# One GpSimd addition in place of two for both heads of a forgetting-attention key tile

## What is computed

```python
logits = jnp.einsum('bthd,bshd->bhts', qi, k).astype(jnp.float32) * ATTN_SCALE
logits = logits + (ci[..., :, None] - c_key[:, :, None, :])
logits = jnp.where(pi[:, None] >= key_pos[None, :], logits, NEG_INF)
probs = jax.nn.softmax(logits, axis=-1)
return jnp.einsum('bhts,bshd->bthd', probs.astype(v.dtype), v)
```

```python
merged = (jax.nn.sigmoid(ga + b_gate[i, 0]) * (y_swa @ w_up_swa[i])
          + jax.nn.sigmoid(gf + b_gate[i, 1]) * (y_fox @ w_up_fox[i]))
h = h + _rmsnorm(merged @ w_out[i], g_post[i])
```

## Time and profile before

| | |
|---|---|
| median of three executions | 843.04 us |
| the three | 843.82, 837.07, 843.04 us |
| the profiled execution | 837.59 us, of it the span from first to last instruction 835.8 us |
| mean granted TensorE clock | 0.992 |

### The profile page before, as it was taken

The page is one execution under the profiler, slowest core; times in us unless marked ns, Lnnn a source line. Parts: engine busy times, 40 slices in busy tenths (PEclk is TensorE's granted clock), DMA queues, the critical chain, the costliest instruction groups (busy, mean ns, idle before and its releaser), DMA issues.

```text
span 835.8 us, 12898 instructions
## 1 busy us (share of the span) xinstructions
PE 802.9 (96%) x4514; PEld 649.0 (78%) x4514; DVE 505.1 (60%) x1050; ACT 315.3 (38%) x645; POOL 350.8 (42%) x292
## 2 busy tenths in 40 slices
PE   3999999999999999999999999999989999999997
PEld 3999999987878878788787865756565688878885
DVE  7944788456676767645646457795878744442222
ACT  6422241333333333333333336666667123222111
POOL 4412224454445435344444324757774344412221
PEclk9999999999999999999999999999998999999999
DMA  9342424569857346355364599999700475342221
GB/s 295 103 127 53 128 65 109 135 164 267 240 164 205 103 140 191 103 165 165 99 178 116 138 239 237 235 240 226 188 2 2 138 224 150 118 174 103 87 91 75
DMA packets 122712, 125.00 MB, mean 150 GB/s; under 512 B 30116, under 2 KB 92404, under 8 KB 122648
## 3 DMA queue, kind: packets, MB, share of 16 engines
q1 hardware_dynamic: 121208, 119.92, 53.7%
q10 hardware_dynamic: 1440, 4.26, 1.4%
HBM read 90.93 MB, written 34.92 MB: 151 GB/s over the span
## 4 chain that ended last, share of the span: by engine, by line
PE 83%; DVE 6%; issue 5%; POOL 3%; ACT 1%; DMA 1%; DVEq 0%; SPq 0%; ACTq 0%; POOLq 0%
PE PS L1857 20%; PE PS L1858 20%; PE PS L1859 20%; PE PS L2106 4%; PE PS L2107 3%; PE PS L2108 3%; PE PS L1964 2%; POOL acc L1220 2%; PE PS L2029 1%; PE PS L2009 1%; PE PS L2044 1%; PE PS L2059 1%; PE PS L2010 1%; PE PS L1879 1%; DMA x_all<-in_x_dram 1%
## 5 line engine op out<-in xcount | busy, mean ns | idle before, releaser
L1151 POOL TENSOR_TENSOR ops<-s_sum,ops 128x512 fp32r<-128x512 f32 x64 | 87.5, 1378 | 111.2 <-ACT ops L1249 111.2
L1857 PE MATMUL PS<-t_hi,ops 128*128 128x512 f32 x256 | 101.1, 395 | 0.0
L1858 PE MATMUL PS<-t_lo,ops 128*128 128x512 f32 x256 | 99.8, 390 | 0.0
L1859 PE MATMUL PS<-t_hi,ops 128*128 128x512 f32 x256 | 99.8, 390 | 0.0
L1151 POOL TENSOR_TENSOR ops<-raw,ops 128x512 fp32r<-128x512 f32 x48 | 65.5, 1365 | 69.0 <-ACT ops L1249 68.9
L1220 POOL TENSOR_TENSOR acc<-acc,p_fox 128x400 f32<-128x400 f32 (+5 forms) x76 | 62.2, 838 | 5.9 <-ACT p_fox L1373 3.6
L1172 POOL TENSOR_TENSOR w_plain<-raw,w_plain 128x1024 fp32r<-128x1024 f32 x10 | 28.0, 2796 | 84.8 <-ACT w_plain L1278 84.8
L1679 DVE TENSOR_TENSOR z_tmp<-u,PS 128x512 f32<-128x512 f32 x48 | 33.0, 686 | 49.2 <-PE PS L1859 28.2
L1249 ACT ACTIVATE ops<-s_sum 128x512 fp32r<-128x512 f32 x64 | 39.6, 623 | 52.8 <-DVE s_sum L1481 41.8
L1373 ACT ACTIVATE p_fox<-PS,neg_c_col 128x512 f32<-128x512 f32 (+5 forms) x112 | 54.2, 534 | 14.0 <-PE PS L2015 7.5
L1859 PEld LDWEIGHTS PS<-t_hi,ops 128*128 128x128 f32 x256 | 48.1, 188 | 10.6
(11 more groups left out here) (205 smaller groups left out, 2176.9 us busy)
## 6 DMA issues: line engine op xcount, KB each, us to landing
raw<-in_w_in_dram SPq DMA_DIRECT2D x34, 512.0 KB, 5.2
q_dram<-stage_b SPq DMA_DIRECT2D x32, 256.0 KB, 3.0
g_dram<-stage_b SPq DMA_DIRECT2D x32, 256.0 KB, 2.0
tanh_g<-g_dram SPq DMA_DIRECT2D x16, 512.0 KB, 3.9
max_k<-k_dram SPq DMA_DIRECT2D x16, 260.0 KB, 5.5
max_c<-neg_c_dram SPq DMA_DIRECT2D x8, 520.0 KB, 6.2
x_all<-in_x_dram SPq DMA_DIRECT2D x8, 512.0 KB, 7.9
raw<-in_w_in_dram SPq DMA_DIRECT2D x16, 256.0 KB, 4.7
```

Source lines behind the costliest of these rows:

```text
L1151: nc.gpsimd.tensor_tensor(ops[:, i % OPS, 1], op_source(p, name), ops[:, i % OPS, 0].bitcast(F32), ALU.subtract).then_inc(op_ready, 1)
L1857: pe.matmul(dst, hi_w, hi, start=first, stop=False)
L1858: pe.matmul(dst, hi_w, lo, start=False, stop=False)
L1859: return pe.matmul(dst, lo_w, hi, start=False, stop=last)
```

## The change

In a unit that isn't shared, GpSimd now handles both heads with one instruction: the two blocks of `acc` and the two neighbouring tiles of the `p_fox` ring are addressed as one operand of two rows. It waits for both heads' exponentials. Shared units are as they were. The counts in `acc_done` follow: a unit with one instruction for both heads counts once, and both its `p_fox` tiles become free with it.

```diff
                 for h in range(2):
-                    who = "dve" if h and st["q"] and st["i"] <= 4 else "pool"
-                    acc_total[who] += 1
+                    shared = st["q"] and st["i"] <= 4
+                    who = "dve" if h and shared else "pool"
+                    acc_total[who] += 1 if shared or not h else 0
...
-                    for h in range(2):
-                        n = 2 * u + h
-                        if acc_by[n] != "pool":
-                            continue
-                        dst = acc[0:keys, f % 2, h, c0:c0 + w]
+                    n = 2 * u
+                    pool.wait_ge(fox_exp, n + 1)
+                    if q == 1 and i <= 4:
+                        dst = acc[0:keys, f % 2, 0, c0:c0 + w]
                         tile = p_fox[0:keys, n % PT_RING, 0:w]
-                        pool.wait_ge(fox_exp, n + 1)
-                        if q == 0 and i == 0:
-                            nc.gpsimd.tensor_copy(dst, tile).then_inc(acc_done["pool"], 1)
-                            continue
-                        other = p_fox[:, (n - 2) % PT_RING, :] if (q, i) == (1, 1) else dst
-                        if n in acc_before:
-                            pool.wait_ge(*acc_before[n])
-                        nc.gpsimd.tensor_tensor(dst, other, tile, ALU.add).then_inc(acc_done["pool"], 1)
+                        other = p_fox[:, (n - 2) % PT_RING, :] if i == 1 else dst
+                    else:
+                        pool.wait_ge(fox_exp, n + 2)
+                        if n + 1 in acc_before:
+                            pool.wait_ge(*acc_before[n + 1])
+                        dst = acc[0:keys, f % 2, :, c0:c0 + w]
+                        tile = p_fox[0:keys, n % PT_RING:n % PT_RING + 2, 0:w]
+                        other = dst
+                    if i == 0:
+                        nc.gpsimd.tensor_copy(dst, tile).then_inc(acc_done["pool"], 1)
+                        continue
+                    if n in acc_before:
+                        pool.wait_ge(*acc_before[n])
+                    nc.gpsimd.tensor_tensor(dst, other, tile, ALU.add).then_inc(acc_done["pool"], 1)
```

## The result

| | kernel before | changed kernel |
|---|---|---|
| median of 22 runs | 838.10 us | 841.60 us |
| lowest to highest | 835.63 to 843.82 | 839.58 to 846.29 |
| span of the profiled execution | 835.8 us | 840.2 us |

The ratio is 1.0041, with a 95% interval from 1.0025 to 1.0057: the changed kernel is slower by 0.4%, or 3.4 us of 838 (2.1 to 4.8 by the interval). That is within the 1% called no change ahead of the result, to which 0.90 was given, and yet larger than the uncertainty of this many runs; 841.6 lies in the range of 837.0 to 849.0. A second measurement of the unchanged pair of kernels gave 1.0040 (1.0011 to 1.0069).

The account below looks back on a forecast made before the run. PE was taken to bound the kernel, waiting mainly for DVE, with GpSimd having some 49 us to spare in attention. 1.2 + 0.6 + 0.2 - 0.1 = +1.9 us on the 843.04 us median gave 844.9 us, range 837.0 to 849.0.

Parts of the forecast that it names:

- What bounds the kernel: Attention: PE is bound and lacks DVE's results; of GpSimd's 2.4 us net saving only 0.1 us counts, at `probs`.
- The price of a pair: GpSimd: one instruction for 2 x 400 columns takes 1.90 us (bounds 1.76 and 2.06) instead of 2.02 for two.
- 621 to 625 us: DVE's `y` split and small operation wait longer behind GpSimd's pairs; PE's 1.91 us pause grows by 1.2 us.
- 645 to 651 us: Before the merge part, the `y` split PE waits for ends later behind a pair: +0.6 us (+0.4 to +0.7).
- The ring: `p_fox` tiles freed together could hold up ACT, tightest at 528 us; cost nothing, covered by an existing wait.
- The wait for both heads: Pairs wait for head 1's exponential, one ACT operation later; cost nothing, covered by `probs`' wait for `rec`.
- 585.6 us: DVE's small operation, blocked by both heads' 144 columns instead of one's, delays the `y` PE awaits: +0.2 us.
- The sum: Whole kernel: 1.2 + 0.6 + 0.2 - 0.1 = +1.9 us, 844.9 us against the median of 843.04.
- The saved time arrives: Rival: PE's pauses hang on GpSimd, so 2.4 to 5.8 us are saved, 837.2 to 840.6 us; chance 0.18.
- DVE blocked everywhere: Rival: pairs double all blocks of DVE's small operations and splits, up to +11.0 us, 854.0 us; chance 0.04.
- Hidden anyway: Rival: PE's pauses shift into each other and the delay disappears, 843.0 us; chance 0.18.
- The slow clock stays longer: Rival: PE's longer pause near 625 us brings 3 to 6 us more half clock, 846.4 to 847.9 us; chance 0.15.

Follow-up runs that it names:

- e6: Kernel before with only the 27 pairs of j = 0 to 2 merged, the last pair of heads left as two instructions: 839.34 us, ratio 0.9997.
- e10: Kernel before with pairs merged only in j = 1, j = 2 and the second half of j = 0, first `y` split two key tiles later: 839.17 us, 1.0005.
- e1: Changed kernel with its joint waits and counts kept, but two GpSimd instructions for a pair again: 840.97 us, ratio 1.0030 to the kernel before.
- e8: Changed kernel with the first split of `y` issued two key tiles later: 839.31 us, ratio 1.0003 to the kernel before.
- e2: Kernel before with only the nine pairs of the last two heads (j = 3) merged: 840.92 us, ratio 1.0033.
- e11: Kernel before with only the first split of `y` two key tiles later, measured a second time: 838.19 us, ratio 0.9984.
- e7: Kernel before with only the first split of `y` two key tiles later, first measurement: 839.04 us, ratio 0.9990.

## Why the prediction was right, and where not

**What bounds the kernel, and that GpSimd's saving is worth nothing on the path:** right. With 27 of 36 pairs merged (e6) or 22 of them (e10) the kernel is no faster. GpSimd's time fell by 4.7 us, where 4 to 6 were forecast, but that it fits is luck: its copies and additions alone went from 72.5 to 65.9 us, 6.6 less, and 1.8 us came back in the projections (L1173), which the change does not touch. In the second profile, without this, its time is 7.1 us lower. The 0.1 us that PE was to gain at its wait for `probs` did not come: it waits 0.28 us there in both kernels.

**The price of a pair:** right. 1.90 us were taken for 2 x 400 columns, and 1.88 to 1.90 us measured where nothing disturbs it; the 544 columns take 1.35 us, so 256 columns more cost 0.54 to 0.56 us, 2.1 to 2.2 ns each. A dependent pair starts 0.23 us after the end of the one before it, where 0.15 had been read from single additions. It happens seven times in each of the two profiles, not ten.

**621 to 625 us, +1.2 us:** right in mechanism and order of the turns, 1.07 us in size. The split was put at about 2.6 us and took 2.58, the pause at 3.1 us and it was 2.98. e1 takes the long hold away and has the 1.90 us of before.

**645 to 651 us, +0.6 us:** right in mechanism, +0.46 us in size. The early split came 0.36 us sooner (forecast 0.3), and the blocked one took 2.18 us and set the start of the merge part.

**The ring, nothing:** right in the changed kernel. At 528 ACT no longer waits, and its waits for `acc` in attention fell from 4.2 to 3.5 us in all. At the end the joint return does delay ACT's last exponentials, so that PE stands 0.46 us longer ahead of the last value matmuls. The forecast did not have this. It stays without effect because the split comes later still. e1 shows the cost when it is not covered: a wait of 2.16 us instead of 0.58.

**The wait for both heads, nothing:** this step failed, a term put at nothing by a cover that is not there at the start. The cover named was `probs`' wait for `rec`. At the start of attention there is no such wait ahead of the first tiles: GpSimd stands idle and takes each exponential as it comes. The copy of two rows starts one exponential later, two dependent starts follow, and the pair is still running when DVE's copies come. That is +0.5 us, measured as 0.52 to 0.65 in all six kernels that merge there or wait jointly, and 0.00 to 0.01 in all five others. The sentence "where GpSimd is there first" named the condition; the place was in the rows from 494 us on, ahead of the stretch that was read.

**585.6 us, +0.2 us:** open. It is +0.34 us in one profile of the changed kernel and in those of e6, e8 and e10, and -0.08 in the other profile of the changed kernel. The pair that DVE met was that of 2 x 272 columns, not that of 2 x 144 which the forecast named.

**The sum.** By the parts 1.9 us were forecast; the three places measure 2.1 us, which is the lower end of what the ratio gives, 2.1 to 4.8. That the two sums agree is partly luck: 0.5 us at the start that had been left out stands against smaller terms elsewhere. Between the 2.1 us and the 3.4 us of the ratio 1.3 us stay open.

The mean clocks say where they may lie. A mean clock lower by 0.0029 over 840 us is some 4.9 us more at half clock in a run, about one and a half stretches of 3.4 us. At 0.9 to 1.6 us for a stretch, as measured below, that is an estimate of 1.3 to 2.3 us. Among the 93 runs of the kernel before, a run with a clock lower by 0.001 is longer by 1.0 us on average, but pauses and slow stretches come together, so that this does not tell cause from effect. Nor do clock and time always go together: e2 has a ratio of 1.0033 with a clock of 0.9903, near that of before. So the slow clock is a likely part of the open 1.3 us and is not shown to be all of it.

The absolute forecast missed by only 3.3 us because two errors partly cancel: it was set on the median of three runs, 4.9 us above that of 22, and the growth was put 1.6 us too small. 838.1 + 1.9 would have been 840.0.

**The rivals.** "The saved time arrives" and "DVE blocked everywhere" did not happen: the small operations take 12.9 us in all where it was 13.0, and the seven long splits 12.4 where it was 10.4. "Hidden anyway" is excluded by the interval. "The slow clock stays longer" did not happen behind the pause itself: half clock followed the pause of 2.98 us for about 7 us, as it followed the 1.91 us of before from 624.6 to 631.4 us (the changed kernel, columns as in the earlier trace rows):

```profile
631.60:638.60 7.00, 6.60 (x28) 5.12 (x28) 4.77 (x19) 4.53 (x14) 2.71 (x4) 0.51 0.00 0
```

Over the whole span and all runs it did happen, as the mean clocks show. So this rival, which had 0.15, came in part, at other places than the one it named.

## What to carry to other kernels

Before you merge two instructions of an engine that has time to spare, ask who is blocked while it runs and who waits for its first half: the gain was some 5 to 7 us of GpSimd's time and worth nothing, the longer hold on DVE and the joint waits cost 2.1 us at three places, and the kernel became 3.4 us slower. Read the start and the end of a stage separately, since the waits that cover a delay in its middle are not there. Set a forecast's difference against the centre of many runs, or the profiled execution, not against three runs that spread more than the effect. And when the places of one profile do not add up to the loss, look at the granted clock of all the runs, and not of one.

## What was not expected of the hardware

**GpSimd blocks even a tiny DVE operation for its whole instruction.** 16 columns from bf16 to f32, one input, take 0.14 us alone, 1.30 us behind 544 columns and 1.52 behind 800; two cast copies of 208 columns took 1.18 us instead of 0.65. In these traces some of DVE's operations were not lengthened while GpSimd ran: the copies of `p_t`, which read PSUM, took at most 0.69 us with it or without it, the reciprocals of 128 columns at most 0.95 us, the reductions over `neg_sink` at most 0.16 us. The Trainium skill, page "SBUF — State Buffer", section "SBUF: two separate sides", says of the ports that these two engines share that the one that starts first "gets the pair for the whole instruction; the other fully blocks". The trace agrees: the split stood behind the pair until its end, 2.58 us instead of 1.22. It adds that the two took turns when both had work waiting.

**One stretch of PE's half clock costs 0.9 to 1.6 us, and it comes in one execution and not in the next.** Two kernels that do the same at the start of attention, e10 and e11, differ there in the granted clock alone (columns as in the earlier trace rows); e10 first:

```profile
506.80:510.20 3.40, 3.40 (x13) 2.40 (x13) 0.17 (x1) 3.40 (x9) 1.76 (x5) 0.51 0.37 90
```

```profile
506.80:510.20 3.40, 3.40 (x23) 1.89 (x24) 1.04 (x6) 3.21 (x9) 0.76 (x3) 1.00 0.75 249
```

The one with 0.51 (1.2 of 2.4 GHz) came 0.88 us later from there on. At 632 us it is the other way about, e11 and then e10, both behind a pause of 2.33 us:

```profile
632.10:634.80 2.70, 2.70 (x15) 1.15 (x12) 1.06 (x3) 1.32 (x3) 1.71 (x2) 0.50 0.02 6
```

```profile
635.00:640.00 5.00, 5.00 (x36) 2.63 (x36) 4.17 (x7) 4.43 (x8) 2.90 (x3) 1.00 0.01 3
```

Here e11 lost 1.63 us. The same kernel as e11, profiled as e7, has the pause of 2.33 us too and full clock behind it. The same pause is thus followed by half clock in one execution and by full clock in another, and a change that adds a pause adds a chance of that as well. By the mean clocks the changed kernel spends more time at half clock than the kernel before. Which of its places brings that on was not tested.
